# The first blocks of a fused two-layer diffusion backbone: another order of first loads, three split weight blocks, and low weights on DVE

## The reference

```python
sc, scc = silu(c), silu(c_ctx)
mod_x = sc @ ada_w[l] + ada_b[l]            # 6 x 1024: shift, scale, gate, twice
mod_c = scc @ ada_w[l] + ada_b[l]           # the same for context tokens
hx = modulate(rms_norm(x, norm1_g[l]), sh1x, sc1x)    # h * (1 + scale) + shift
hc = modulate(rms_norm(ctx, norm1_g[l]), sh1c, sc1c)
gq, gkk, gv, gg, lr_f, lr_b, bq, bk, bv = split_cols(h @ w_in, EVEN_WIDTHS)
dec_f = log_sigmoid(lr_f @ gk_w[0] + gk_b[0]) / 16    # and dec_b, for the gated scan
# then gated linear attention (8 heads) beside grouped attention (8 heads) -> w_out,
# gated residual, SwiGLU; layer 1: windowed attention with sinks, SwiGLU; final norm
```

## Time and profile before

| | |
|---|---|
| median of 3 runs | 1628.85 us |
| profiled execution, its own time | 1632.49 us |
| its span, mean granted clock | 1630.7 us, 0.988 |
| PE busy | 1563.8 us, 96% |
| DVE busy | 894.4 us, 55% |
| ACT busy | 544.6 us, 33% |
| POOL busy | 590.3 us, 36% |
| weight blocks | 181 loads of 512 KB |

### The profile page before, as it was taken

The page is one execution under the profiler, slowest core; times in us unless marked ns, Lnnn a source line. Parts: engine busy times, 40 slices in busy tenths (PEclk is TensorE's granted clock), DMA queues, the critical chain, the costliest instruction groups (busy, mean ns, idle before and its releaser), DMA issues.

```text
span 1630.7 us, 25138 instructions
## 1 busy us (share of the span) xinstructions
PE 1563.8 (96%) x10712; PEld 1289.3 (79%) x10712; DVE 894.4 (55%) x1250; ACT 544.6 (33%) x711; POOL 590.3 (36%) x264
## 2 busy tenths in 40 slices
PE   6999998879999999999999999999999999999997
PEld 3888764367888888888888888855569998998995
DVE  5699776568577766665466433657633321221324
ACT  4743424453422211221122233245544221222232
POOL 1263335602333322222322223245644444444442
PEclk9999999999999999999999999999999999999998
DMA  8523110034233333334433222200012223223232
GB/s 337 196 103 117 41 39 1 1 132 142 67 117 128 130 129 124 116 123 138 147 130 115 90 68 65 72 20 1 1 52 91 91 93 101 91 91 103 91 101 93
DMA packets 41775, 158.54 MB, mean 97 GB/s; under 512 B 4768, under 2 KB 5152, under 8 KB 39872
## 3 DMA queue, kind: packets, MB, share of 16 engines
q1 hardware_dynamic: 41232, 156.74, 27.9%
q0 software_dynamic: 432, 0.20, 0.1%
HBM read 154.95 MB, written 2.10 MB: 96 GB/s over the span
## 4 chain that ended last, share of the span: by engine, by line
PE 71%; DVE 4%; issue 2%; ACT 1%; POOL 1%; DVEq 0%; POOLq 0%
PE psum L1708 65%; PE psum L1908 2%; PE psum L1878 1%; DVE osb L1301 1%; PE psum L1811 1%; POOL acc L593 1%; DVE mx L1196 0%; PE psum L1923 0%; DVE product L1066 0%; PE psum L1895 0%; PE psum L1882 0%; PE psum L1884 0%; PE psum L1880 0%; PE psum L1761 0%; DVE xT L1539 0%
## 5 line engine op out<-in xcount | busy, mean ns | idle before, releaser
L1708 PE MATMUL psum<-act,whi 128*128 128x258 f32 (+2 forms) x4000 | 793.7, 319 | 7.1 <-DVE xT L1539 4.5
L619 POOL TENSOR_TENSOR wlo<-raw,whi 128x1024 fp32r<-128x1024 f32 (+1 forms) x181 | 441.7, 2440 | 918.5 <-ACT whi L650 918.5
L1708 PEld LDWEIGHTS psum<-act,whi 128*128 128x128 f32 x4000 | 594.0, 189 | 67.9 <-issue 13.5
L1708 PE MATMUL psum<-act,wlo 128*128 128x512 f32 (+1 forms) x2000 | 477.4, 317 | 0.0
L1066 DVE SCALAR_TENSOR_TENSOR product<-adr,cb 128x1024 f32<-128x1024 f32 x128 | 285.7, 2264 | 132.6 <-DMA adr<-adat_dram 127.3
L1708 PEld LDWEIGHTS psum<-act,wlo 128*128 128x128 f32 x2000 | 312.2, 190 | 27.4
L650 ACT ACTIVATE whi<-raw 128x1024 fp32r<-128x1024 f32 (+1 forms) x181 | 188.0, 1039 | 328.1 <-DMA raw<-weights_dram 328.0
L1114 DVE SCALAR_TENSOR_TENSOR tmps<-psum,rs 128x256 f32<-128x256 f32 (+1 forms) x176 | 78.0, 484 | 196.5 <-PE psum L1708 191.9
L1708 PE MATMUL psum<-gh,wlo 128*128 128x512 f32 (+1 forms) x528 | 160.9, 359 | 0.0
L1708 PE MATMUL psum<-gh,whi 128*128 128x512 f32 (+1 forms) x528 | 160.9, 358 | 0.0
L1708 PE MATMUL psum<-gl,whi 128*128 128x512 f32 (+1 forms) x528 | 159.4, 355 | 0.0
(11 more groups left out here) (183 smaller groups left out, 1220.0 us busy)
## 6 DMA issues: line engine op xcount, KB each, us to landing
raw<-weights_dram SPq DMA_DIRECT2D x181, 512.0 KB, 3.5
adr<-adat_dram SPq DMA_DIRECT2D x80, 512.0 KB, 4.5
ada_w<-ada_dram SPq DMA_DIRECT2D x8, 1024.0 KB, 15.5
xT<-x_in_dram SPq DMA_DIRECT2D x4, 1536.0 KB, 13.4
cb<-crow_dram SPq DMA_DIRECT2D x2, 1024.0 KB, 8.4
out_dram<-big SPq DMA_DIRECT2D x8, 256.0 KB, 2.1
con<-consts_dram SPq DMA_DIRECT2D x1, 512.0 KB, 7.4
con<-consts_dram SPq DMA_DIRECT2D x1, 320.0 KB, 4.0
```

The source lines that it names most:

```text
L619: nc.gpsimd.tensor_tensor(wlo[:, s, 0:w], raw[:, s, 0:w], whi[:, s, 0:w].bitcast(F32), ALU.subtract).then_inc(sem("s_lo"), 1)
L1708: last = MM(out_[:, o:o + t1 - t0], w_, a_[:, t0:t1], start=k == order[0] and j == 0, stop=k == order[-1] and j == 2)
```

## The change

The first loads come in another order: the first half of the modulation weights, weight block 0, then the latent part of x for tiles 0 to 3, weight blocks 1 and 2, the next modulation weights, the latent part of tiles 4 to 7, and the context part of all tiles last. `gkw` is loaded ahead of the activated c's rows. Three blocks instead of two are split (block 2's result goes to `wk[1]`), and the split runs over halves of the tiles: as soon as modulation group 0 is there, `modA` is made for tiles 0 to 3, and the products with them start; those of groups 1 to 3 are put between. In blocks 0 to 18 DVE makes `wlo` (`weights_low`), behind the evacuation of the block two before; POOL does so from block 19 on. The logits and what hangs on them move from blocks 2 and 3 to 3 and 4, `low_rank_low` from block 2 to 3, and the decays from ahead of the evacuation of blocks 5 and 6 to behind it. ACT's high part of block 3 moves ahead of the low-rank copies.

```diff
@@ -421,9 +421,11 @@
+first_out = [lin[0], lin[1], wk[1]]
+
 def out_parts(n, tok):
-    ps = lin[n % 2]
+    ps = first_out[n] if n < 3 else lin[n % 2]
     if tok == T:
@@ -529,21 +531,24 @@
     x_tiles = x_in.rearrange("p (k t) -> p k t", k=KT)
-    for h in range(ADA_RING):
-        load_ada(h)
+    load_ada(0)
+    load_ada(1)
     load_raw(0)
-    sp.dma_start(xT[:, 0:half, :], x_tiles[:, 0:half, :]).then_inc(sem("s_xa"), 16)
-    sp.dma_start(xT[:, half:KT, :], x_tiles[:, half:KT, :]).then_inc(sem("s_xb"), 16)
+    sp.dma_start(xT[:, 0:half, 0:NX], x_tiles[:, 0:half, 0:NX]).then_inc(sem("s_xa"), 16)
     load_raw(1)
+    load_raw(2)
+    load_ada(2)
+    load_ada(3)
+    sp.dma_start(xT[:, half:KT, 0:NX], x_tiles[:, half:KT, 0:NX]).then_inc(sem("s_xb"), 16)
+    sp.dma_start(xT[:, :, NX:T], x_tiles[:, :, NX:T]).then_inc(sem("s_xc"), 16)
     for h in range(ADA_RING, 2 * len(ADA_EARLY)):
         load_ada(h)
-    load_raw(2)
     sp.wait_ge(sem("s_adamm"), 2 * len(ADA_EARLY))
+    sp.dma_start(gkw[0:32, :], gkw_in).then_inc(sem("s_rope"), 16)
     load_c()
...
     sp.dma_start(con[:, 0:CC_ID], consts[:, 0:CC_ID]).then_inc(sem("s_rope"), 16)
-    sp.dma_start(gkw[0:32, :], gkw_in).then_inc(sem("s_rope"), 16)
     for n in range(RING, NB):
@@ -615,9 +620,10 @@
         w = BLOCKS[n]["nk"] * P
-        pool.wait_ge(sem("s_hi"), n + 1)
-        nc.gpsimd.tensor_tensor(wlo[:, s, 0:w], raw[:, s, 0:w], whi[:, s, 0:w].bitcast(F32),
-                                ALU.subtract).then_inc(sem("s_lo"), 1)
+        if n >= FIRST[("out", 0)]:
+            pool.wait_ge(sem("s_hi"), n + 1)
+            nc.gpsimd.tensor_tensor(wlo[:, s, 0:w], raw[:, s, 0:w], whi[:, s, 0:w].bitcast(F32),
+                                    ALU.subtract).then_inc(sem("s_lo"), 1)
         if n == 16:
@@ -693,20 +699,23 @@
     ada_copy(0)
-    ada_copy(1)
     high(0)
-    act.wait_ge(sem("s_modA"), 1)
     for k in range(KT):
         if k % 4 == 0:
+            act.wait_ge(sem("s_modA"), 2 if k else 1)
             act.wait_ge(sem("s_xb" if k else "s_xa"), 16)
...
             .then_inc(sem("s_nhx"), 1)
-    high(1)
+        if k == 3:
+            high(1)
+            high(2)
+            ada_copy(1)
+    act.wait_ge(sem("s_xc"), 16)
     for k in range(KT):
...
     for k in range(KT):
-        if k == 2:
+        if k == 4:
             ada_copy(2)
@@ -793,15 +802,14 @@
             nc.scalar.preload_act_table_set(LN_EXP)
-        if n in (2, 3):
-            logits(2 * n - 4)
-            logits(2 * n - 3)
-        if n in (2, 3):
-            minus_exponential(2 * n - 4)
-            minus_exponential(2 * n - 3)
         if n in (3, 4):
-            logarithm(2 * n - 6)
-            logarithm(2 * n - 5)
+            logits(2 * n - 6)
+            logits(2 * n - 5)
+            minus_exponential(2 * n - 6)
+            minus_exponential(2 * n - 5)
+        if n in (4, 5):
+            logarithm(2 * n - 8)
+            logarithm(2 * n - 7)
         if n in (7, 8):
@@ -975,7 +983,8 @@
             attention(1)
-        high(n + 2)
+        if n >= 2:
+            high(n + 2)
         if (kind, L) in NORM_FOR and n == FIRST[(kind, L)] and n > 0:
@@ -991,6 +1000,8 @@
                 mixer_projection(L, n, b)
+            if n == 0:
+                high(RING)
             if L == 0:
@@ -1115,16 +1126,27 @@
     dve.wait_ge(sem("s_par"), 16)
-    for c in range(2):
-        ada_reduce(c)
-    dve.wait_ge(sem("s_mod"), 2)
-    mod_scale(0)
-    dve.wait_ge(sem("s_modA"), 1)
-    for k in range(KT):
-        hi, lo = [act_tile("proj", 0, k, low) for low in range(2)]
-        dve.wait_ge(sem("s_nhx"), k + 1)
-        STT(out=lo[:, 0:NX], in0=xT[:, k, 0:NX], scalar=modA[:, 0, k, 0:1], in1=hi[:, 0:NX].bitcast(F32),
-            op0=ALU.mult, op1=ALU.subtract).then_inc(sem("s_nlx"), 1)
+    def weights_low(n):
+
+        s = n % RING
+        dve.wait_ge(sem("s_hi"), n + 1)
+        TT(wlo[:, s, :], raw[:, s, :], whi[:, s, :].bitcast(F32), ALU.subtract).then_inc(sem("s_lo"), 1)
+
+    for h in range(2):
+        ada_reduce(h)
+        dve.wait_ge(sem("s_mod"), h + 1)
+        mod_scale(0, 4 * h, 4 * h + 4)
+        if h == 0:
+            weights_low(0)
+        dve.wait_ge(sem("s_modA"), h + 1)
+        for k in range(4 * h, 4 * h + 4):
+            hi, lo = [act_tile("proj", 0, k, low) for low in range(2)]
+            dve.wait_ge(sem("s_nhx"), k + 1)
+            STT(out=lo[:, 0:NX], in0=xT[:, k, 0:NX], scalar=modA[:, 0, k, 0:1], in1=hi[:, 0:NX].bitcast(F32),
+                op0=ALU.mult, op1=ALU.subtract).then_inc(sem("s_nlx"), 1)
+        if h == 0:
+            weights_low(1)
+            weights_low(2)
     for k in range(KT):
@@ -1133,9 +1155,10 @@
             dve.wait_ge(*nq("sq", 0, 1))
+        if k == 4:
+            ada_reduce(2)
         add_square(0, k, T)
-    for c in range(2, 4):
-        ada_reduce(c)
+    ada_reduce(3)
     dve.wait_ge(sem("s_shift"), 1)
@@ -1394,13 +1417,8 @@
-        if n == 2:
+        if n == 3:
             low_rank_low()
-        if n in (5, 6):
-            for i in (2 * n - 10, 2 * n - 9):
-                decays(i)
-            for i in (2 * n - 10, 2 * n - 9):
-                references(i)
         if n in (7, 8):
@@ -1556,6 +1574,8 @@
             dve.wait_ge(*nq("rs", q, 1))
+        if 2 <= n <= FIRST[("out", 0)] - 2:
+            weights_low(n + 1)
         if kind == "proj" and L == 0:
@@ -1589,6 +1609,11 @@
                     late_modulation(i)
+            if n in (5, 6):
+                for i in (2 * n - 10, 2 * n - 9):
+                    decays(i)
+                for i in (2 * n - 10, 2 * n - 9):
+                    references(i)
         if kind == "proj" and L == 1:
@@ -1644,23 +1669,23 @@
-        if c >= 2:
-            pe.wait_ge(sem("s_adacp"), c - 1)
+        if c >= 1:
+            pe.wait_ge(sem("s_adacp"), c)
         for half in range(2):
...
             for g in range(4):
-                last = MM(wk[0][32 * g:32 * g + 32, 512 * (c % 2):512 * (c % 2) + 512],
+                last = MM(wk[0][32 * g:32 * g + 32, 0:512],
                           cpad[:, 4 * half + g, :], ada_w[:, h % ADA_RING, g, :], start=half == 0,
...
         pe.wait_ge(sem("s_adacp"), c + 1)
-        if c >= 2:
-            pe.wait_ge(sem("s_mod"), c - 1)
+        if c >= 1:
+            pe.wait_ge(sem("s_mod"), c)
         for q in range(4):
-            last = TR(wk[1][:, 512 * (c % 2) + P * q:512 * (c % 2) + P * q + P],
+            last = TR(wk[0][:, 512 + P * q:512 + P * q + P],
                       adasb[:, c % 2, q * P:q * P + P], ident)
@@ -1764,18 +1791,25 @@
     ada_mm(0)
+    ada_T(0)
+    first_blocks(0, 0, range(0, 4))
     ada_mm(1)
-    ada_T(0)
+    first_blocks(1, 0, range(0, 2))
     ada_T(1)
-    first_blocks(0, 0)
+    first_blocks(1, 0, range(2, 4))
+    first_blocks(2, 0, range(0, 4))
+    first_blocks(0, 0, range(4, 8))
     ada_mm(2)
-    first_blocks(1, 0)
+    first_blocks(1, 0, range(4, 6))
+    ada_T(2)
+    first_blocks(1, 0, range(6, 8))
     ada_mm(3)
-    ada_T(2)
+    first_blocks(2, 0, range(4, 6))
     ada_T(3)
+    first_blocks(2, 0, range(6, 8))
     mean_square(0, T)
-    first_blocks(0, 1)
-    first_blocks(1, 1)
+    for n in range(3):
+        first_blocks(n, 1)
@@ -1991,9 +2025,11 @@
-        if n in (2, 3):
-            logits(2 * n - 4)
-            logits(2 * n - 3)
+        if n in (3, 4):
+            logits(2 * n - 6)
+            if n == 3:
+                pe.wait_ge(*ev(2))
+            logits(2 * n - 5)
         if n == 9:
```

More of the change, by code:

```diff
@@ L1074, in late_bias, with mod_scale @@
                     .then_inc(sem("s_mod"), 1)
[L1076 removed]
+            def mod_scale(a, k0=0, k1=KT):
                 layer, second = divmod(a, 2)
                 c0 = 32 if second else 8
[L1080 to L1081 removed]
+                gain = par[:, PC_N + KT * a + k0:PC_N + KT * a + k1].unsqueeze(2).to_broadcast([P, k1 - k0, 2])
+                STT(out=modA[:, a, k0:k1, :], in0=mod[:, layer, c0 + k0:c0 + k1, :], scalar=1.0, in1=gain, op0=ALU.add,
                     op1=ALU.mult).then_inc(sem("s_modA"), 1)
@@ L1710, in block_products, with first_blocks @@
                 last.then_inc(sem("s_acc"), 1)
-            def first_blocks(n, part):
-                out_ = lin[n % 2]
+            def first_blocks(n, part, tiles=range(KT)):
+                out_ = first_out[n]
                 t0, t1 = ((0, NX), (NX, TX))[part]
@@ L1720, in first_blocks @@
                     pe.wait_ge(sem("s_shift"), 2)
-                for k in range(KT):
+                for k in tiles:
                     if n == 0:
@@ L2159, in _ @@
                     first_outputs(n)
-                elif n >= 2 and n != FIRST[("out", 0)] + 1:
+                elif n >= 3 and n != FIRST[("out", 0)] + 1:
                     block_products(n)
```

13 lines of the change are left out of this document (6 added, 7 removed).

## The result

The kernel became slower, by a little: a median of 1634.24 us (6 runs, 1631.49 to 1637.26) against 1628.63 (6 runs beside them). The ratio is 1.0038, with a 95% interval of 1.0024 to 1.0052, so 3.9 to 8.5 us. The forecast was no change. The profiled execution took 1634.97 us (span 1633.1).

A forecast was written before the change was run, and what follows sets the result against it. PE was taken as the bound, so time moves only where it idles or runs at the lower clock. Terms -4.4 + 7.2 + 2.1 - 8.1 + 2.0 + 0.6 = -0.6 us gave 1628.3 us, range 1619 to 1635.

The forecast's parts named there:

- signs of being right: First product 17 to 18, block 2's end 53 to 55, logits stop 5 to 9, half clock, no block 8 stop, sums 1.2.
- term 4: DVE lacks slack: POOL's scan subtractions delay blocks 7 and 8's low weights, 2.0 us lost; block 17's added subtraction, 0.6 lost.
- term 3: Blocks 5 to 13: low weights on DVE and later decays remove PE's stops and clock loss, 8.1 us gained.
- Term 1: Head to block 2's end: first product near 17.2 instead of 24.0, half clock counted again, 4.4 us gained.
- Term 2: Behind block 2: logits and block 4 wait behind DVE's sums needing activated c; 7.2 us stop, 2.1 half clock.
- No stop, or a short one: Rival, behind block 2: the queue makes no stop or a short one without lower clock; 1619.0 or 1621.3 us; chance 0.27.
- DVE the bound in blocks 6 to 12: Rival: POOL's subtractions and products stand in front of DVE's work; 1633.7 us with half of them; chance 0.18.
- The head gains nothing: Rival, at the start: loads of x in shorter rows land later, 3 us of 4.4 lost, 1631.3 us; chance 0.10.

The follow-up runs named there:

- e2: The changed kernel, with POOL's subtraction for block 19 waiting until DVE's product of the states in block 17 is done; 1627.96 us, ratio 1.0001.
- e9: e8 plus POOL's subtraction for block 19 waiting for DVE's product of the states in block 17; 1623.26 us, ratio 0.9969 to the kernel before.
- e8: The kernel before, with only DVE making low weights of blocks 3 to 18 and decays behind the evacuations of blocks 5 and 6; 1626.23 us, ratio 0.9979.
- e3: The changed kernel, with c activated right behind the first root and the logits' low halves made ahead of the late sums; 1626.14 us, ratio 0.9985.
- e5: The changed kernel, with only the logits' low halves moved ahead of the late sums, c activated where the change has it; 1632.24 us, ratio 1.0013.
- e7: The changed kernel with both e2's wait on POOL and e3's early c and low halves; 1621.93 us, ratio 0.9955 to the kernel before.

## Why the prediction was wrong

The forecast was a sum of -0.6; by the last mark it was 5.7, and the terms as read one by one give 5.5. Term by term, in us (less than zero is a gain):

| term | forecast | measured |
|---|---|---|
| 1 head, to the end of block 2 | -4.4 | -5.1 |
| 2 queue behind block 2: stops | +7.2 | +7.1 and +2.0 |
| 2 half clock behind it | +2.1 | +2.1 |
| 3 stops and clock loss gone | -8.1 | -7.4 |
| 4 new waits, blocks 5 to 12 | +2.0 | +1.1 |
| 4 block 17 | +0.6 | +5.7 |
| sum | -0.6 | +5.5 |

Without the last term the forecast is -1.2 and the measured sum -0.2, but that is in part luck: the terms above it are off by -0.7, +1.9, +0.7 and -0.9, and offset each other. The prediction's signs of being right came nearly all (first product, end of block 2, stop ahead of the logits, half clock, sums at 1.2; only the wait ahead of block 8 was not to come), and they all lie ahead of block 17, where they could not have shown the failure.

**The step that failed** is the last sentence of term 4: "In block 17 DVE has another 1.15 ahead of the maximum that PE waits for, with half of it idle before: 0.6 lost, bounds 0 and 1.2." It priced the added instruction by its own duration, less what is idle. The kernel before had at this very place two instructions that started 0.22 us apart and were in each other's way, and DVE was the one that came first. To move DVE by 1.1 us turned that round. This could have been read: the rows at 212.10 (2.70) and 212.32 (4.67) stood in the trace of before, and the prediction had in term 3 the price of coming second. It looked for such meetings in blocks 5 to 12 and not behind them. An upper bound that follows from its own numbers is the added 1.15 and POOL's 2.4, some 3.5 us, and not 1.2; the maximum came 3.1 later. e2 shows this cause: it leaves the added work and takes away the meeting, and the 6 us are gone; e9 does the same to e8. Of the 5.7, 2.7 are the stop (0.7 for the added work, as forecast, and 2.0 for the meeting); 3.0 are the clock, which e8 shows to be no sure consequence. For the meeting, and for the clock in block 17, the prediction had put nothing.

**Term 1** was right in kind and 0.7 too small. The first product starts at 17.16 (forecast 17.2). The half clock that it counted again, 2.1, came as half speed: PE's first nine products last to 20.98, 3.8 us in place of 2.1 at 0.23 each. The windows there give a granted clock of 1.00 all the same; the kernel before has the same pace from 23.99 on, with 0.50 in its windows.

**Term 2** was right in its mechanism and its place, with two errors that offset each other in the stop. c was ready at 61.1, later by 1.7 than the chain had it, because block 3's weights, issued at 47.65, were there for ACT only at 52.92: 5.3 us, not the median of 3.5. But that late load also made PE start block 3 later, by a wait of 1.96 that the prediction did not have, so the stop ahead of the logits is 7.07 all the same, and the two together are 9.0. The half clock was there: 0.50 from 72 to 74, 0.65 in the next window. e3 and e5 show the chain.

```profile
72.00:74.00 2.00, 2.00 (x8) 1.71 (x8) 2.00 (x5) 0.53 (x1) 0.00 (x0) 0.50 0.13 51
74.00:76.00 2.00, 2.00 (x10) 1.74 (x9) 2.00 (x5) 2.00 (x4) 0.00 (x0) 0.65 0.27 37
```

**Term 3**: of the four stops, those at blocks 5 and 11 are gone with the clock loss behind the latter (0.9, 1.9 and 1.7), that at block 13 is 0.66 in place of 2.09, and the one ahead of block 8 is a new one (1.07). Counted as 7.4 gained here (with the old 1.5 ahead of block 8) and the 1.07 under term 4. e8 and e9 show the gain by itself: from the first logits to the transposes in block 13 each is 5.9 us shorter than before, where terms 3 and 4 had 8.1 less 2.0.

**Term 4, first part**, was right in its mechanism and too large: one wait of 1.1, ahead of block 8, where 2.0 were forecast. DVE works without a gap from 100.24 until it has made block 8's low weights (108.48, 1.22 us), and one of its decays on the way took 2.26 in place of 0.95, beside POOL's two subtractions on scans (from 98.69, 4.00 us):

```profile
101.25 2.26 DVE L1383 SCALAR_TENSOR_TENSOR dec<-dec,gsc 128x768 f32<-128x768 f32 x1
```

**The rivals.** "No stop, or a short one" fell with the row at 71.13; as e3 it is now a kernel, at 1626.1, and not at 1619, since it still has block 17's stop; without that, as e7, it is at 1621.9. "DVE the bound in blocks 6 to 12" had the right mechanism, POOL's instruction in front of DVE's; in those blocks it cost 1.1 us, and the loss came in block 17. It comes nearest to what happened, but that its number fits is chance: it gave 1633.7 with half of the operations, and 1634.2 was measured, by another sum. "The head gains nothing" fell: 5.1 us ahead at the end of block 2.

What stays open: why the clock falls for long behind one stop of 2.69 us (the change), for less behind the same stop in e3 and e5, and not at all in e8; and why the load of block 3 took 5.3 us. No run tried either.

## What to carry to other kernels

Before you add or move an instruction on VectorE, look for every place behind it where a VectorE and a GpSimd instruction on SBUF start close together, and ask which of them is first afterwards; the price of coming second was 2.0 us here and 2.2 in the earlier trace rows, nearly the length of the other's instruction, and the cure is a wait on the engine that has time (here one line, 6 us with the clock behind it). When you put early work on an in-order queue, follow the operand that comes last to everything queued behind it: here a new order of the users alone only moved the stop, and with the late producer (c) moved too it was gone. And compare marks, the same instruction in both traces, all the way to the end of the edited part; sums that agree at the first marks can still be wrong behind them.
